# mLSTM heads taken in pairs between dense tiles, in a two-block fp32 transformer kernel

## The reference, cut to what matters

```
proj = h @ w_in                         # q, k (8 heads x 64), v (8 x 128), o_pre (1024), gates (16)
f_log = log_sigmoid(gates[8:])          # i_log = gates[:8]
b = cumsum(f_log);  logD = b_l - b_s + i_s  (s <= l)
m_l = max over s of logD;  D = exp(logD - m_l)
s = (q k^T / 8) * D
num = s @ v;  den = sum_s s
h_out = num / max(|den|, exp(-m_l))
h_out = h_out * rsqrt(mean(h_out^2) + eps) * g_head       # per head, over its 128 columns
out = (sigmoid(o_pre) * h_out) @ w_out
```

## Time and profile before

| | us |
|---|---|
| median of three runs (2134.53 to 2137.72) | 2134.98 |
| profiled execution | 2137.02 |
| its span, first to last instruction | 2135.3 |
| PE busy in it | 2060.6 (97%) |
| DVE, ACT, POOL busy | 1089.7, 713.1, 31.8 |

### The profile page before, as it was taken

One profiled execution on the slowest core, in us unless ns is written; L12 is line 12 of the kernel. 1 busy time (PEld: TensorE's weight loads), 2 busy tenths in 40 slices (PEclk: granted clock), 3 DMA queues, 4 the chain that ended last, 5 costly groups with the idle time before them and its releaser, 6 DMA issues.

```text
span 2135.3 us, 24366 instructions
## 1 busy us (share of the span) xinstructions
PE 2060.6 (97%) x9451; PEld 1612.8 (76%) x9451; DVE 1089.7 (51%) x1426; ACT 713.1 (33%) x1001; POOL 31.8 (1%) x61
## 2 busy tenths in 40 slices
PE   7999989999999999989999999899999979999998
PEld 5984467888888777767888888666668857888887
DVE  4334655542556444555543555765644566543544
ACT  4223433221224344433222234345442333222222
POOL 0000000000000000000000001000100000000000
PEclk9997799999999999999999999999999989999999
DMA  3320023324224322132334325211422313333322
GB/s 124 106 93 20 0 60 98 94 82 120 79 76 125 111 83 80 45 94 79 93 91 112 98 74 138 79 42 58 94 60 80 108 48 99 93 89 94 99 74 84
DMA packets 297846, 180.14 MB, mean 84 GB/s; under 512 B 22168, under 2 KB 294657, under 8 KB 297769
## 3 DMA queue, kind: packets, MB, share of 16 engines
q1 hardware_dynamic: 297752, 179.08, 29.4%
q10 hardware_dynamic: 16, 0.02, 0.0%
HBM read 176.85 MB, written 2.20 MB: 84 GB/s over the span
## 4 chain that ended last, share of the span: by engine, by line
PE 90%; DVE 5%; ACT 3%; issue 1%; SPq 0%; DMA 0%; ACTq 0%; DVEq 0%
PE psum L1337 26%; PE psum L1339 26%; PE psum L1338 26%; PE psum L1498 2%; PE psum L1671 1%; PE psum L1649 1%; DVE wl L871 1%; PE psum L1451 1%; PE psum L1529 1%; PE psum L1460 1%; PE psum L1676 1%; PE psum L1473 1%; PE psum L1506 1%; PE psum L1511 1%; ACT wh L559 1%
## 5 line engine op out<-in xcount | busy, mean ns | idle before, releaser
L871 DVE TENSOR_TENSOR wl<-stage,wh 128x2048 fp32r<-128x2048 f32 (+3 forms) x178 | 369.4, 2076 | 149.6 <-ACT wh L559 149.0
L559 ACT CAST wh<-stage 128x2048 fp32r<-128x2048 f32 (+3 forms) x178 | 306.2, 1721 | 229.9 <-PE psum L1339 223.5
L1337 PE MATMUL psum<-xl,wh 128*128 128x512 f32 x864 | 351.6, 407 | 10.5 <-DVE xl L886 9.6
L1339 PE MATMUL psum<-xh,wh 128*128 128x512 f32 x864 | 338.6, 392 | 0.0
L1338 PE MATMUL psum<-xh,wl 128*128 128x512 f32 x864 | 338.2, 391 | 0.0
L1337 PE MATMUL psum<-x2l,wh 128*128 128x512 f32 x768 | 303.6, 395 | 7.3 <-DVE wl L871 7.3
L1339 PE MATMUL psum<-x2h,wh 128*128 128x512 f32 x768 | 300.0, 391 | 0.0
L1338 PE MATMUL psum<-x2h,wl 128*128 128x512 f32 x768 | 299.9, 391 | 0.0
L1337 PEld LDWEIGHTS psum<-xl,wh 128*128 128x128 f32 x864 | 163.5, 189 | 70.8 <-issue 31.9
L1337 PE MATMUL psum<-hidl,wh 128*128 128x512 f32 x528 | 205.8, 390 | 2.6 <-DVE wl L871 2.6
L1339 PE MATMUL psum<-hidh,wh 128*128 128x512 f32 x528 | 205.4, 389 | 0.0
(11 more groups left out here) (255 smaller groups left out, 2517.3 us busy)
## 6 DMA issues: line engine op xcount, KB each, us to landing
stage<-in_ffn_w_gate_dram SPq DMA_DIRECT2D x44, 512.0 KB, 4.0
stage<-in_ffn_w_up_dram SPq DMA_DIRECT2D x44, 512.0 KB, 5.2
stage<-in_w_in_dram SPq DMA_DIRECT2D x40, 512.0 KB, 4.2
stage<-in_a_w_in_dram SPq DMA_DIRECT2D x24, 512.0 KB, 4.6
stage<-in_ffn_w_down_dram SPq DMA_DIRECT2D x32, 384.0 KB, 3.9
stage<-in_w_gate_dram SPq DMA_DIRECT2D x22, 512.0 KB, 4.0
stage<-in_w_up_dram SPq DMA_DIRECT2D x22, 512.0 KB, 5.2
stage<-in_ffn_w_down_dram SPq DMA_DIRECT2D x32, 320.0 KB, 3.8
```

The costliest lines, as they stand in the source:

```text
L559: nc.scalar.copy(wh[:, par, 0:n], stage[:, par, 0:n]).then_inc(w_hi, 1)
L871: vec.tensor_tensor(wl[:, par, 0:n], stage[:, par, 0:n], wh[:, par, 0:n].bitcast(F32), ALU.subtract).then_inc(w_lo, 1)
L1337: mm(out, a_hi, b_lo, start=start, stop=False)
L1339: return mm(out, a_hi, b_hi, start=False, stop=stop)
```

## The change

Mixer A is put on a stream like B and C. Its dense blocks become `A_q0, A_k0, A_v0` (plain), then a stream of `o0, v1, o1, q1, k1, o2, v2, v3, o3` and `A_outA` (K = 768), cut into 23 phases by `A_RATE`; `A_outB` (K = 256) follows by `linear`. Heads go in pairs p = 0..3, five phases each; the tail of pair p (squares, normalization, gate, split) stands in phases 0 and 1 of pair p+1. The values and denominators of the pair's second head stand half a phase's dense units behind the first's. The two spreading products of a head become fp32r ones with 40 rows (8 rows of the high part, 8 of the rest at partition 32, zeros between). D is made in `pt` itself. The DVE reciprocal is replaced by ln and exp on ACT, and the gate's sigmoid by its logarithm (abs, exp, ln on ACT, one DVE instruction), which is added before one exp. The gated heads go to `ygh`, `ygl`.

```diff
+    for name in ("q0", "k0", "v0", "o0", "v1", "o1", "q1", "k1", "o2", "v2", "v3", "o3"):
+        add(f"A_{name}", {"v": "tokens", "o": "gate"}.get(name[0], "copy"), 1)
+    add("A_outA", "partial", 4, kt=6)
+    add("A_outB", "residual", 4, kt=2, squares=True)
...
+A_PAIRS, A_PHASES = A_HEADS // 2, 5
+A_RATE = [6, 9, 7, 7, 15, 7, 9, 7, 7, 16, 7, 9, 7, 7, 13, 6, 9, 7, 7, 14, 6, 5, 5]
...
 # ACT, stream part of attention_a
+                for s in range(len(A_RATE)):
+                    p, j = divmod(s, A_PHASES)
...
+                    if j == 4:
+                        for a in range(2):
+                            e = 2 * p + a
+                            act.wait_ge(a_den, e + 1)
+                            nc.scalar.activation(dn[:, a, :], psum[:, 7 - 2 * a, :], ACT.Abs).then_inc(a_abs, 1)
+                            act.wait_ge(a_max, e + 1)
+                            nc.scalar.activation(dn[:, a, :], dn[:, a, :], ACT.Ln).then_inc(a_lnd, 1)
+                            act.wait_ge(a_lnd, e + 1)
+                            nc.scalar.activation(dn[:, a, :], dn[:, a, :], ACT.Exp, scale=-1.0).then_inc(a_r, 1)
+                            act.wait_ge(a_hs, e + 1)
...
+                            nc.scalar.activation(hq[:, a, :], hs[:, a, :], ACT.Square).then_inc(a_sq, 1)
+                    for b in a_stream.splits(s):
+                        split_of(b)
...
 # DVE
+                    def blocks_of_phase():
+                        if s >= 1:
+                            for b in a_stream.ended[s - 1]:
+                                epilogue_of(b)
+                        for b in a_stream.splits(s - 1):
+                            split_of(b)
...
+                    if j == 0 and p >= 1:
+                        dve.wait_ge(o_ready, p)
+                        for a in range(2):
+                            e = 2 * p - 2 + a
+                            dve.wait_ge(a_ln, e + 1)
+                            vec.scalar_tensor_tensor(out=dn[:, a, :], in0=dn[:, a, :], scalar=-0.5, in1=og[:, e, :],
+                                                     op0=ALU.mult, op1=ALU.add).then_inc(a_t, 1)
...
+                    blocks_of_phase()
 # PE
+                    def values(a):
+                        for t in range(TT):
+                            mm(psum[:, 6 - 2 * a, t * P:S], av[:, 2 * p + a, t, :], pt[:, a, t, 0:S - t * P],
+                               start=(t == 0), stop=(t == TT - 1))
+                        for t in range(TT):
+                            last = mm(psum[:, 7 - 2 * a, t * P:S], ones[:, :], pt[:, a, t, 0:S - t * P],
+                                      start=(t == 0), stop=(t == TT - 1))
+                        last.then_inc(a_den, 1)
...
+                        if j == 4:
+                            pe.wait_ge(a_p, 8 * p + 8)
+                            pe.wait_ge(block_out, st[f"A_v{p}"].b0 + 1)
+                            values(0)
+                    if j == 0 and p >= 1:
+                        pe.wait_ge(a_abs, 2 * p)
+                        for a in range(2):
+                            pe.wait_ge(a_sq, 2 * p - 1 + a)
+                            mm(psum[:, 5 - a, :], ones[:, :], hq[:, a, :], start=True, stop=True).then_inc(a_ss, 1)
+                    units_of(a_stream, s, 0, 2)
+                    if j == 4:
+                        values(1)
+                    units_of(a_stream, s, 1, 2)
+                linear("A_outB")
```

More of the change, by code:

```diff
@@ L165, in build @@
     b_names = [n for n in st if n[:2] == "B_" and n not in ("B_k0", "B_q0", "B_outB")]
+    a_names = [n for n in st if n[:2] == "A_" and n not in ("A_q0", "A_k0", "A_v0", "A_outB")]
     c_names = [f"C_{q}{c}" for c in ("a1", "b0", "b1") for q in "qkv"] + ["C_ga"]
@@ L448, in load_stage @@
                     return
-                if s.b0 == 0:
-                    for j in range(s.blocks // 2):
-                        load(s, name, j, 0)
-                        load(s, name, j, 1)
-                else:
-                    with nc.sync.Fori(0, s.blocks // 2) as j:
-                        load(s, name, j, 0)
-                        load(s, name, j, 1)
+                with nc.sync.Fori(0, s.blocks // 2) as j:
+                    load(s, name, j, 0)
+                    load(s, name, j, 1)
             for t in range(TT):
@@ L1253, in _ @@
-            linear("A_o")
-            dve.wait_ge(o_out, 4)
-            def probabilities(h, tiles):
-                for t in tiles:
-                    g = TT * h + t
-                    dve.wait_ge(a_s, g + 1)
-                    dve.wait_ge(a_mask, g + 1)
-                    if h >= 2:
-                        dve.wait_ge(a_den, h - 1)
-                    n = S - t * P
-                    vec.scalar_tensor_tensor(out=pt[:, h % 2, t, 0:n], in0=psum[:, 4 + g % 2, 0:n], scalar=SCALE,
-                                             in1=work[:, t, 0:n], op0=ALU.mult, op1=ALU.mult).then_inc(a_p, 1)
@@ L1643, in scores @@
-            def scores(h, tiles):
-                rows = slice(A_DQK * (h % 2), A_DQK * (h % 2) + A_DQK)
-                for t in tiles:
-                    g = TT * h + t
-                    if g >= 2:
-                        pe.wait_ge(a_p, g - 1)
-                    mm(psum[:, 4 + g % 2, 0:S - t * P], qk[rows, 4 + h // 2, t * P:(t + 1) * P],
-                       qk[rows, h // 2, t * P:S], start=True, stop=True).then_inc(a_s, 1)
-            def head_squares(e):
-                pe.wait_ge(a_sq, e + 1)
-                mm(psum[:, 2 + e % 2, :], ones[:, :], hq[:, :], start=True, stop=True).then_inc(a_ss, 1)
@@ L1681, in _ @@
-            linear("A_out", between=(3, lambda: head_squares(A_HEADS - 1)))
+            attention_a()
             feed_forward(0)
```

499 lines of the change are left out of this document (284 added, 215 removed).

## The result

The changed kernel takes 2101.89 us (median of 4 runs, 2099.83 to 2105.33) where the kernel before takes 2135.82 us (4 runs, 2134.53 to 2137.72) on the same chip: a ratio of 0.9835, 95% interval 0.9824 to 0.9847. It is 1.65% faster. Forecast were 2101 us and a range of 2088 to 2114. The profiled execution took 2103.34 us with a span of 2101.6 us. Lines 1410 to 1412 of the kernel after are the three products of a dense unit (1337 to 1339 before), line 915 is DVE's part of the weight split (871 before).

The account below looks back on a forecast made before the run. PE was taken as the bound everywhere, working slowly in mixer A's head loop. 115.8 us go and 62.3 + 4.4 + 1.0 + 1.6 + 13.0 = 82.3 come, saving 33.5: about 2101 us, range 2088 to 2114.

Parts of the forecast that it names:

- Head work at full clock: PE's values, denominators, squares, scores, spreads, changes and transposes in mixer A come back at full clock: 62.3 us.
- Spreads 0.23 us each: Mixer A's 16 spreads, one fp32r product each, priced by type and columns: 3.7 us, at most 13.8.
- Scores 11.9 us: Mixer A's paired heads' scores overlap mostly, not fully: 3.0 us a pair, 11.9 in all, between 8.6 and 17.2.
- Changes 5.0 us: PE's switches between dense and head work: 0.2 us at each of 25 places, 5.0 us, between 0 and 8.
- Block waits 4.4 us: PE waits for late weight splits: 2.0 us at q1, 0.8 at v2, 1.6 at `A_outA`'s last block; between 0 and 12.
- Clock 1.0 us: One low-clock spell of a few microseconds may follow the 2.0 us wait: 1 us, between 0 and 5.
- Start 1.6 us: DVE's wait for the `gf` copy delays block 2 by 1.0 us, PE's wait for `g_step` adds 0.6; between 0 and 4.
- End 13.0 us: `A_outB`'s short blocks lose 13.0 us in waits and low clock before the norm's sum, as in mixer B; 8 to 15.
- 1 (cover complete, 2092 us): Splits come in time, no clock is lost, scores overlap fully: 4.4 + 1.0 + 3.3 us less, 2092 us; chance 0.20.
- 2 (2112 us): Head chain late in every phase, or block waits twice as long with a low spell at each: 2112 us; chance 0.21.
- 3 (2166 us): Head products pull the clock down wherever they stand, so mixer A's stage runs at 0.75: 2166 us; chance 0.03.
- 4 (2125 us): PE waits at phase 4 for values and `pt` until dense units end up in a row: 2125 us; chance 0.04.

Follow-up runs that it names:

- repeat: The changed kernel run once more, unaltered, against the kernel before: 2100.76 us, ratio 0.9827.
- wider last step: The changed kernel with `A_outA` and `A_outB` at 4 k-tiles each instead of 6 and 2, v2 put before o2: 2094.65 us.
- 128-row run: The kernel before with the spreads' three 8-row tiles widened to 128 rows, 120 of them zero: 2125.55 us, 0.9952 of the kernel before.
- kernel without cover: The changed kernel with its unit table altered so that phases 2 to 4 of each pair have no dense units: 2165.96 us.

## Why the prediction was right

The forecast held: 2101 us against 2101.89, and the sum 33.5 us against 34.8 in the profiled executions. PE was the bound and at a low clock, and the stage now runs at 0.99, as forecast. Two things in it were luck. The prediction took the full clock from mixer B's stage, where head work stands among dense products; what held it down was the 8 rows of the spreads, which the change replaces as well, and which the prediction priced only as products of another type. And errors of opposite sign cancelled: scores 3.3 us too dear, changes 2.7 too cheap, the start 0.7 too dear, the clock 0.7 too cheap. That the median came within a microsecond says nothing of how exact the terms are. Step by step:

- **What bounds it: right, with one wrong reason.** PE at half clock in the head loop. The additional "wait for `pt` behind the reciprocal" does not exist: without the reciprocal the value products take 4.34 us as before. It carried no term, since the prediction took the loop as a whole (114.8 us).
- **Head work at full clock, 62.3 us: measured 61.7.** The stage from 67.0 to 266.9 us is 199.9 us; less the dense products' 132.6 (as before), the three waits' 4.3 and 1.7 us of half clock leaves 61.3, and 0.4 for the transposes. The scores and the changes in it were off and cancelled. With the scores at 8.6 us and the other terms as summed, 7.7 us are left for the 25 changes, 0.3 us each on average. The single ones of the scores cost 0.4.
- **Spreads 0.23 us each: right**, the term with the widest bounds (to 13.8 us). In fp32 they cost 10.0 us more, and the kernel took 2111.89 us.
- **Scores 11.9 us: mis-sized, 8.6.** The 1.06 us for a pair of 512 came out, but the prediction read the 0.2 us above 0.86 as overlap that is missing, and it is the change to the dense product, which it counts once more among the changes. The Trainium skill says that different tiles of the array can work in parallel ("TensorEngine Tiling (Array Packing)", Key Properties); the run with the scores apart agrees, fully, with one head at 0.84 us and two at 0.85.
- **Changes 5.0 us: mis-sized, nearer 8.** The same section says that changing the tiling mode drains the engine. The 0.4 us of a single change may be that; no run here tells it from the change of type.
- **Block waits 4.4 us: measured 2.08 + 0.72 + 1.54 = 4.3**, for the stated reason, which the reordered DVE shows by taking all three away. The prediction also foresaw where they stand.
- **Clock 1.0 us: mis-sized, 1.7.** One spell, 119.8 to 123.2 us, 3.4 us at 1.2 GHz behind the 2.08 us wait. The waits of 0.72 and 1.54 us had none. In the repeat, and in the runs with the wider last step and with the scores apart, the same 2.08 us wait was followed by full clock. The prediction read the Trainium skill ("TensorE: Matmul & The Clock Gate", HAM oscillation) to mean that each of the three waits would cost a spell, 2105 us; that did not come about. The page's own example has waits of about 3 to 5 us, longer than these, so this case is no test of it.
- **Start 1.6 us: mis-sized, 0.9.** The copy of `gf` landed 2.1 us after its issue, at 50.5 us, yet PE started block v0 at 54.01 us as before. Of the two parts only PE's wait for `gnx` came.
- **End 13.0 us: right.** 35.0 us from start to norm sum, 34.8 in mixer B, and the wider cut shows the cause: it leaves 3.6 us of the loss.
- **The rivals.** 1 (cover complete, 2092 us) did not come: the splits were late. Its waits and its clock are what DVE's changed order brings, 2093.67 us. Its third part, the full overlap of the scores, was there all along and is in both times. 2 (2112 us) needed waits in every phase, and there are three. 3 (2166 us) was against the rows, and the 128-row run says why: the change replaces the products that held the clock down. The change with 8-row spreads was not run, so whether dense neighbours alone would have kept the clock is open. The 128-row run shows that they are not needed for it: the clock is 0.97 there without any. 4 (2125 us) did not come: no wait for `pt` stands in the stage. The kernel without cover took 2166 us as well, but by another way than rival 3, and it is no test of it.

What the change brought can be told apart now. The loop's 114.8 us held 8 heads of about 9.0 us at full clock (5376 columns a head at 0.86 us for 512) and the 0.4 us of transposes, some 72.5 us. Against the 61.7 us of after these are some 11 us less: spreads 10 and scores 8.6 less, changes 8 more. The other 42 us were 28 of half clock (55.7 us of it in 166.2 to 285.1 us), 8.5 us of idle time (118.9 less 110.4 busy), and 6 us that I cannot place. All of them went. The two causes need each other: with the clock back but no dense work beside the heads the loop gains 12.4 us, since ACT and DVE then set its pace. Given back were waits and clock at the pair's start (6.0), the start (0.9) and the end (13.0).

## What to carry to other kernels

When an engine is both the bound and at a low clock, look for the instruction that fills few of its rows before blaming its waits; widening an operand with zeros is a cheap test. When short chains are laid between long blocks, walk the other engines' queues for what stands ahead of the next block's preparation: one pair of instructions in the wrong place cost up to 7 us here, and was found in the order, not in the busy shares. And split a layer's contraction so that its last part still covers its own preparation.

## What the runs showed of the hardware beyond that

- Products over 8 rows held TensorE's granted clock at 0.75 of full over 108 us; the same over 128 rows, 120 of them zero, left it at 0.97 with more idle time in the stretch.
- 512 columns took 0.86 us as fp32 and 0.23 us as fp32r also with 40 rows, the change to dense work on top (1.91 and 0.66 us for two).
- Two products of 64 rows on different halves of the rows took the time of one: 0.85 us for the 384 columns of two heads with the change behind them, 0.84 us for those of one. A change from dense work to scores and back cost 0.4 us.
- A DVE reciprocal of 128x512 took 3.35 us, logarithm and exp of the same on ACT 0.63 each, 1.3 us together.
- Half clock followed some waits and not others: 3.4 us of it behind 2.08 us in one execution and none in another of the same kernel, none behind 0.72 and 1.54 us. What decides it the runs do not settle.
